# S5 mixer of a two-block transformer: four state units at a time on the TensorE array, and two of VectorE's six modulation operations given to GpSimd

## The chip, the cores and the metric

The kernel runs on one core of one Trainium2 chip. The metric is device time in microseconds (us) of one execution, the median of several runs. The change is judged against the kernel before.

## The reference

The program is two transformer blocks over 512 tokens of width 1024 in float32. The second block has three mixers side by side (RWKV-7, S5, gated linear attention), then cross attention and a convolutional feed-forward. The change touches only S5, a complex diagonal state space model with 32 groups of 16 channels and 64 states each:

```
bu_re = einsum('blgc,gnc->blgn', uf, bbar_re)
bu_im = einsum('blgc,gnc->blgn', uf, bbar_im)
_, _, s_re, s_im = lax.associative_scan(_complex_affine_combine,
                       (abar_re, abar_im, bu_re, bu_im), axis=1)
y = (einsum('blgn,gcn->blgc', s_re, c_re) - einsum('blgn,gcn->blgc', s_im, c_im) + d * uf)
y = gelu(y)
y = y * sigmoid(y @ w_glu + b_glu)
```

## The kernel before

The weights of both blocks stream from memory as 512 KB units through a ring of five buffers in SBUF. SyncE issues these loads as the ring comes free. TensorE works almost without a break; the other engines prepare what it reads and take away what it wrote. One stage of the program, `s5_inputs`, holds the S5 recurrence together with the projections of the second block.

The S5 states are worked as units of 128 partitions (two channel groups, 64 states each). There are 16 of them for each half of the sequence (256 tokens). VectorE takes them two at a time: one q is two units (index e) over one half a, so q runs from 0 to 15. In the rest of this text such a q is called a pair.

For a pair, the steps are:

- `inputs(q)` on TensorE, L2772 to L2784: bu for both units, real and imaginary part. That is 4 matmuls with a contraction of 32 rows. The two units sit in two different 32-row groups of the array. Each matmul writes 256 columns of a PSUM bank. The pair takes banks 0 and 1 or banks 2 and 3, in turn.
- The modulation on VectorE, L2888 to L2895: four products of bu with cosine and sine tables (`er`, `ei`), and then a sum and a difference of these products. Each is 128 partitions by 512 elements. The factors come from PSUM and SBUF; the sum and difference read only SBUF.
- Four `tensor_tensor_scan` of 256 elements (L2903), real and imaginary part of two units.
- Four products that turn the scanned states back (L2908 to L2911), into the buffer `o[:, q % 2]`.
- `outputs(q)` on TensorE, L2786 to L2798: 8 matmuls with 32 output columns each, accumulated four deep. The two units write two different 32-partition strips of one bank.
- After every second pair `s5_skip` (L2929) adds d * u and takes the bank's result.

Each float32 matmul shows as two MATMUL and two LDWEIGHTS records in the trace, so 8 matmuls are 16 records.

Between these TensorE issues steps of the projections, from the generator `side`: one step is one 128x512 matmul. There are 120 steps: 88 from `contract_steps` (L1059) and 32 from `token_steps` (L2966). The order is written out by hand:

```
inputs(0)
inputs(1)
for q in range(16):
    for _ in range(8):
        next(side, None)
    outputs(q)
    if q + 2 < 16:
        inputs(q + 2)
```

ScalarE copies the projections out of banks 6 and 7 and applies the gelu at the end. GpSimd has nothing in this stage; its next work is two memsets of the following stage (L3152, L3153), after the last `outputs`. Stages follow each other without a barrier; only semaphores order them.

Of the kernel before, what the change touches and what calls it, by code (L numbers as in the profile page):

```python
# [17 lines left out]
ALU = mybir.AluOpType  # L18
# [309 lines left out]
class Signal:  # L328
# [13 lines left out]
    def now(self):  # L342
# [12 lines left out]
           'r_t', 'r_tok', 'r_tt', 'r_turned', 'r_u', 'r_u0', 'r_u0p', 'r_vb', 'r_w',  # L355
           'r_wp',
           'w_sum', 'w_p', 'w_p1', 'w_u', 'w_c', 'w_c11', 't_sum', 'd_x', 'd_freed', 's5_bt', 'conv_gate', 'conv_up',
           's5_loaded', 's5_in', 's5_mod', 's5_dem', 's5_out', 's5_y', 's5_glu',
           'g_in', 'g_neg', 'g_soft', 'g_cum', 'g_exp', 'g_dec', 'g_turned', 'g_kt', 'g_scored', 'g_att', 'g_intra', 'g_inter',
           'x_p', 'x_add', 'x_g', 'm_in', 'm_sq', 'm_sum', 'm_ln', 'm_root', 'm_ready', 'k_p', 'k_out', 'q_p', 'q_out', 'v_p',  # L360
           'x_sum', 'x_ln', 'x_root', 'prescaled', 'g_upd', 'g_st', 'g_y', 'g_add', 'g_sq', 'g_sum', 'g_ms', 'g_ln', 'g_root', 'g_gate']
# [596 lines left out]
class Net:  # L958
# [1788 lines left out]
    def s5_inputs(self, down, both, square, t, u, y, qk, go, gd, v, m, z, o, cneg):  # L2747
# [12 lines left out]
        with self.phase() as block:  # L2760
            @block.tensor
            def _(pe):
                def columns():
                    for i in range(2, len(dense)):
                        if i == 3:
                            pe.wait_ge(*s['s5_u'].at(2))
                        elif i >= 4:
                            pe.wait_ge(*s['freed'].at(i - 3))
                        yield from self.contract_steps(pe, ps[:, 6 + i % 2, :], h, s['projected'], i == 2)
                    yield from self.token_steps(pe, [6, 7], h, s['projected'], s['freed'], len(dense) - 2)  # L2770

                def inputs(q):  # L2772
                    a, p = pairs[q]
                    if q >= 2:
                        pe.wait_ge(*s['s5_mod'].at(q - 1))
                    if a == 0 and p % 2 == 0:
                        i = p // 2
                        pe.wait_ge(*(s['s5_u'].at(i + 1) if i < 2 else s['freed'].at(i - 1)))
                    for j in range(2):
                        for e in range(2):  # L2780
                            r, i = rows(2 * p + e), p // 2
                            mm = pe.matmul(ps[:, 2 * (q % 2) + e, half * j:half * (j + 1)], t.bt[r, j, i * P:(i + 1) * P],
                                           u[r, i, half * a:half * (a + 1)], start=True, stop=True)
                    mm.then_inc(*s['s5_in'].up())  # L2784

                def outputs(q):  # L2786
                    a, p = pairs[q]
                    i = p // 2
                    pe.wait_ge(*s['s5_dem'].at(q + 1))
                    if p % 2 == 0 and 4 * a + i >= 2:  # L2790
                        pe.wait_ge(*s['s5_y'].at(4 * a + i - 1))
                    c = lambda e: slice(32 * (2 * p + e), 32 * (2 * p + e) + 32)
                    for j in range(4):
                        for e in range(2):
                            w = (t.big[:, 2, c(e)], cneg[:, c(e)], t.big[:, 3, c(e)], t.big[:, 3, c(e)])[j]
                            mm = pe.matmul(ps[rows(2 * p + e), 4 + i % 2, 0:half], w, o[:, q % 2, j, e, :],  # L2796
                                           start=(j == 0), stop=(j == 3))
                    mm.then_inc(*s['s5_out'].up())  # L2798

                down.pe(pe)  # L2800
                self.contract(pe, ps[:, 2, :], h, s['projected'], deferred=True, ready='x_g')
                pe.wait_ge(*s['accumulated'].at(DT - 1))
                self.root_pe(pe, 0)
                pe.matmul(ps[:, 1, :], self.c('ones'), self.root[:, :], start=True, stop=True).then_inc(*s['y_sum'].up())
                pe.wait_ge(*s['d_freed'].at(4))
                self.contract(pe, ps[:, 7, :], h, s['projected'])
                side = columns()
                inputs(0)
                inputs(1)
                for q in range(16):  # L2810
                    for _ in range(8):
                        next(side, None)
                    outputs(q)
                    if q + 2 < 16:
                        inputs(q + 2)
                for _ in side:
                    pass

            self.s5_end, self.y_read = s['s5_out'].at(16), [s['s5_y'].at(7), s['s5_y'].at(8)]
            self.v_read = [s['freed'].at(len(dense) + k) for k in (1, 2)]  # L2820

            @block.scalar
# [25 lines left out]
            def _(dve):  # L2848
# [30 lines left out]
                for k in range(DT):  # L2879
                    dve.tensor_tensor(h[k], h[k], self.root[:, :], ALU.mult).then_inc(*s['prepared'].up())  # L2880
                dve.tensor_scalar(cneg[:, :], t.big[:, 2, :], -1.0, None, ALU.mult).then_inc(*s['vec'].up())
                for q, (a, p) in enumerate(pairs):
                    g = 2 * p
                    er, ei = t.er[:, g:g + 2, :], t.ei[:, g:g + 2, :]
                    dve.wait_ge(*s['s5_in'].at(q + 1))
                    b = 2 * (q % 2)
                    re, im = ps[:, b:b + 2, 0:half], ps[:, b:b + 2, half:2 * half]
                    dve.tensor_tensor(m[:, 0, :, :], re, er, ALU.mult).then_inc(*s['vec'].up())  # L2888
                    dve.tensor_tensor(m[:, 1, :, :], im, ei, ALU.mult).then_inc(*s['vec'].up())
                    dve.tensor_tensor(m[:, 2, :, :], im, er, ALU.mult).then_inc(*s['vec'].up())  # L2890
                    dve.wait_ge(*s['vec'].now())
                    dve.tensor_tensor(m[:, 3, :, :], re, ei, ALU.mult).then_inc(*s['s5_mod'].up())
                    dve.tensor_tensor(m[:, 0, :, :], m[:, 0, :, :], m[:, 1, :, :], ALU.add).then_inc(*s['vec'].up())
                    dve.wait_ge(*s['s5_mod'].at(q + 1))
                    dve.tensor_tensor(m[:, 2, :, :], m[:, 2, :, :], m[:, 3, :, :], ALU.subtract).then_inc(*s['vec'].up())  # L2895
                    dve.wait_ge(*s['vec'].now())
                    if q:
                        dve.wait_ge(*s['s5_dem'].at(q))
                    for j in range(2):
                        for e in range(2):  # L2900
                            mag = t.fac[:, 0, g + e:g + e + 1].to_broadcast([P, half])
                            first = t.init[:, j, g + e:g + e + 1] if a else 0.0
                            dve.tensor_tensor_scan(z[:, j, e, :], mag, m[:, 2 * j, e, :], first, ALU.mult,  # L2903
                                                   ALU.add).then_inc(*s['vec'].up())
                    if q >= 2:
                        dve.wait_ge(*s['s5_out'].at(q - 1))
                    dve.wait_ge(*s['vec'].now())
                    dve.tensor_tensor(o[:, q % 2, 0, :, :], z[:, 0, :, :], er, ALU.mult).then_inc(*s['vec'].up())  # L2908
                    dve.tensor_tensor(o[:, q % 2, 1, :, :], z[:, 1, :, :], ei, ALU.mult).then_inc(*s['vec'].up())
                    dve.tensor_tensor(o[:, q % 2, 2, :, :], z[:, 0, :, :], ei, ALU.mult).then_inc(*s['vec'].up())  # L2910
                    dve.tensor_tensor(o[:, q % 2, 3, :, :], z[:, 1, :, :], er, ALU.mult).then_inc(*s['s5_dem'].up())  # L2911
                    if a == 0:
                        dve.tensor_copy(t.end[:, :, g:g + 2], z[:, :, :, half - 1]).then_inc(*s['vec'].up())
                    if q == 7:
                        self.s5_turn_state(dve, t)
                    if q >= 2 and p % 2 == 0:
                        self.s5_skip(dve, q // 2 - 1, u, y)
                self.s5_skip(dve, 7, u, y)

            @block.sync  # L2920
            def _(sync):
                self.prefetch(sync)

    def s5_skip(self, dve, k, u, y):

        a, i = divmod(k, 4)
        t = slice(256 * a, 256 * (a + 1))
        dve.wait_ge(*self.s['s5_out'].at(2 * k + 2))
        dve.scalar_tensor_tensor(out=y[:, i, t], in0=u[:, i, t], scalar=self.v('s5_d', i), in1=self.ps[:, 4 + i % 2, 0:256],  # L2929
                                 op0=ALU.mult, op1=ALU.add).then_inc(*self.s['s5_y'].up())  # L2930

# [403 lines left out]
    def second_block(self, down, both, square):  # L3335
        p = self.place
        y_s5, y_gla, qk, go = (p(n, [P, 4, S], 8 * i) for i, n in enumerate(('y_s5', 'y_gla', 'gla_qk', 'gla_go')))
        gd, v, u = p('gla_gd', [P, S], 32), p('gla_v', [P, 4, S], 34), p('u_s5', [P, 4, S], 42)
        self.s5_inputs(down, both, square, self.s5_tables, u, y_s5, qk, go, gd, v, p('s5_m', [P, 4, 2, 256], 50), p('s5_z', [P, 2, 2, 256], 58),
                       p('s5_o', [P, 2, 4, 2, 256], 62), p('s5_cneg', [P, S], 78))  # L3340
        rkv, low = p('rkv', [P, 12, S], 50), p('low_rw', [P, 2, S], 74)
        self.gla_beside_rwkv(u, y_s5, y_gla, qk, go, gd, v, rkv, low)
# [73 lines left out]
```

## Time and profile before

| | us |
|---|---|
| median of 3 runs | 2916.47 (2916.03 to 2916.61) |
| profiled execution, its own time | 2917.33 |
| span of its trace | 2916.0 |
| TensorE matmul busy | 2858.7 (98%) |
| TensorE weight load busy | 1961.6 (67%) |
| VectorE busy | 1619.2 (56%) |
| ScalarE busy | 652.4 (22%) |
| GpSimd busy | 5.0 (0%) |

The spans of the engines overlap. PE is the matmul part of TensorE, PEld its weight load, DVE is VectorE, ACT is ScalarE, POOL is GpSimd and SP is SyncE. A share of 98% holds for the whole span; the stage of the change lies between 1574.9 and 1737.6 us.

### The profile page before, as it was taken

What the parts mean: (1) busy time and instruction counts of PE and PEld (TensorE: products, weight loads), DVE (VectorE), ACT (ScalarE), POOL (GpSimd) and SP (SyncE); (2) the same over time, 40 slices, a digit from 0 to 9 for tenths busy, and PEclk for the clock granted to TensorE, in tenths of its full rate; (3) what the DMA queues carried; (4) which work ended last, traced back from release to release, by engine and by line L of the source; (5) the groups of instructions that cost most, each with busy time, mean ns of one, the idle gap of its engine ahead of it and who ended that gap; (6) DMA issues with size and microseconds to landing.
All of it is one profiled execution on the core that took longest, in us unless ns stands there. A gap on an engine that the chain in (4) does not pass through costs nothing.

```text
span 2916.0 us, 36187 instructions
## 1 busy us (share of the span) xinstructions
PE 2858.7 (98%) x14760; PEld 1961.6 (67%) x14760; DVE 1619.2 (56%) x3196; ACT 652.4 (22%) x1347; POOL 5.0 (0%) x22
## 2 busy tenths in 40 slices
PE   8999999999999999999998999999999999999998
PEld 3567588888544575888885445455554875688886
DVE  5675544453336855466746984455452633666654
ACT  5651300000136513100000021422220102222200
POOL 0000000000000000000000000000000000000000
PEclk9999999999999999999999999999999999999999
DMA  4013122222211231222221111211112331222222
GB/s 146 29 51 101 51 94 87 87 99 97 80 60 49 73 109 66 94 73 87 88 100 65 51 58 58 72 45 45 45 45 93 110 108 46 78 90 89 88 87 80
DMA packets 61941, 224.25 MB, mean 77 GB/s; under 512 B 6992, under 2 KB 7248, under 8 KB 61264
## 3 DMA queue, kind: packets, MB, share of 16 engines
q1 hardware_dynamic: 61776, 221.94, 22.7%
q8 instruction: 117, 1.92, 0.3%
q14 instruction: 48, 0.39, 0.0%
HBM read 219.82 MB, written 2.10 MB: 76 GB/s over the span
## 4 chain that ended last, share of the span: by engine, by line
PE 93%; DVE 6%; issue 1%; ACT 0%; DMA 0%; SPq 0%; DVEq 0%; ACTq 0%
PE ps L1636 29%; PE ps L647 18%; PE ps L1059 15%; PE ps L1047 8%; PE ps L1112 4%; PE ps L1418 3%; PE ps L1391 2%; PE ps L1074 2%; PE ps L1403 2%; PE ps L2796 1%; PE ps L2102 1%; PE ps L2123 1%; PE ps L2319 1%; PE ps L2966 1%; PE ps L1717 1%
## 5 line engine op out<-in xcount | busy, mean ns | idle before, releaser
L1059 PE MATMUL ps<-h,ring 128*128 128x512 f32 x784 | 362.5, 606 | 0.0
L1636 PE MATMUL ps<-h,ring 128*128 128x256 f32 x1136 | 270.7, 381 | 8.5 <-DVE u L1658 4.6
L1059 PEld LDWEIGHTS ps<-h,ring 128*128 128x128 f32 x784 | 143.1, 191 | 159.5 <-issue 153.5
L1636 PEld LDWEIGHTS ps<-h,ring 128*128 128x128 f32 x1136 | 215.9, 191 | 44.0 <-issue 8.7
L1636 PE MATMUL ps<-h_sums,w_sums 128*128 128x256 f32 x1008 | 224.4, 379 | 0.0
L1636 PEld LDWEIGHTS ps<-h_sums,w_sums 128*128 128x128 f32 x1008 | 191.5, 190 | 26.0
L647 PE MATMUL ps<-hid_sums,d_sums 128*128 128x256 f32 x720 | 171.2, 379 | 1.0 <-DVE hid_sums L1595 1.0
L647 PEld LDWEIGHTS ps<-hid_sums,d_sums 128*128 128x128 f32 x720 | 136.6, 190 | 20.3 <-issue 1.8
L1577 DVE TENSOR_TENSOR d_sums<-ring 128x512 f32<-128x512 f32 (+1 forms) x48 | 31.5, 656 | 172.0 <-DMA ring<-stream_dram 172.0
L1112 PE MATMUL ps<-o_x,ring 128*128 128x512 f32 x256 | 112.2, 593 | 0.0
L1636 PE MATMUL ps<-c_h_sums,c_sums 128*128 128x256 f32 x504 | 112.2, 379 | 0.0
L757 ACT ACTIVATE d_xsq<-x 128x512 f32<-128x512 f32 x42 | 24.9, 620 | 368.2 <-DVE x L723 368.2
L1403 PEld LDWEIGHTS ps<-constants,probs 128*128 128x128 f32 x560 | 62.4, 140 | 63.1 <-DVE probs L1525 47.5
L1636 PEld LDWEIGHTS ps<-c_h_sums,c_sums 128*128 128x128 f32 x504 | 95.8, 190 | 13.0
L1457 ACT ACTIVATE probsT<-ps 128x512 f32<-128x512 f32 (+2 forms) x176 | 82.8, 508 | 96.3 <-PE ps L1403 95.8
L1047 PE MATMUL ps<-h,ring 128*128 128x512 f32 x224 | 97.6, 592 | 0.0
L1403 PE MATMUL ps<-constants,probs 128*128 128x128 f32 x560 | 82.7, 279 | 10.4 <-DVE probs L1525 9.6
L1112 PEld LDWEIGHTS ps<-o_x,ring 128*128 128x128 f32 x256 | 48.3, 190 | 60.8 <-issue 58.8
L647 PE MATMUL ps<-hid_sums,ring 128*128 128x256 f32 x360 | 85.5, 379 | 0.0
L647 PE MATMUL ps<-hid,ring 128*128 128x256 f32 x352 | 82.5, 379 | 0.0
L647 PE MATMUL ps<-hid,d_sums 128*128 128x256 f32 x352 | 82.5, 379 | 0.0
L3302 DVE SCALAR_TENSOR_TENSOR c_conv<-c_x,vectors,c_conv 128x511 f32<-128x511 f32 (+1 forms) x88 | 62.1, 747 | 34.1 <-ACT c_conv L3254 33.3
(613 smaller groups left out, 4739.3 us busy)
## 6 DMA issues: line engine op xcount, KB each, us to landing
ring<-stream_dram SPq DMA_DIRECT2D x395, 512.0 KB, 3.7
bias<-bias_dram SPq DMA_DIRECT2D x8, 448.0 KB, 4.3
mem<-mem_dram SPq DMA_DIRECT2D x3, 1024.0 KB, 5.0
x<-x_dram SPq DMA_DIRECT2D x4, 512.0 KB, 7.5
out_dram<-x SPq DMA_DIRECT2D x8, 256.0 KB, 2.2
rope_ab<-ropes_dram SPq DMA_DIRECT2D x4, 256.0 KB, 8.6
s_big<-s_big_dram SPq DMA_DIRECT2D x1, 1024.0 KB, 6.9
constants<-constants_dram SPq DMA_DIRECT2D x1, 768.0 KB, 11.5
```

Of the source, the lines that this page charges most:

```text
L647: mm = pe.matmul(self.region(q, at), w(j), x(k), start=opens, stop=last and j == len(ks) - 1, skip_group_check=True)
L1047: mm = pe.matmul(out, w, r, start=(k == 0), stop=(k == len(rhs) - 1))
L1059: mm = pe.matmul(out, w, r, start=(k == 0), stop=(k == len(rhs) - 1))
L1074: mm = pe.matmul(out, l, w, start=(k == 0), stop=(k == len(lhs) - 1))
L1112: mm = pe.matmul(self.ps[:, m % 4, :], self.next_block(pe), src[k], start=(k == 0), stop=(k == len(src) - 1))
L1391: mm = pe.matmul(ps[:, bank(u, j), 0:(k1 - k0) * P], gr.q[j][i][:, qt * P:(qt + 1) * P], gr.k[j][i][:, k0 * P:k1 * P], start=(i == 0), sto ...
L1403: mm = pe.transpose(ps[:, turn_bank(u, j), b * P:(b + 1) * P], pr[:, u % 3, j, b * P:(b + 1) * P], self.c('ident'))
L1418: mm = pe.matmul(ps[at:at + rows, to, c], gr.v(b, j)[i], pt[:, p % 2, j, b, c], start=(b == 0), stop=(b == nk - 1), skip_group_check=True)
L1457: ins = act.activation(pt[:, p % 2, j, k0:k1, qt * P:(qt + 1) * P], ps[:, turn_bank(u, j), 0:(k1 - k0) * P].rearrange("p (b q) -> p b q", ...
L1577: dve.tensor_tensor(s1, a21, a22, ALU.add).then_inc(*s['vec'].up())
L1636: mm = pe.matmul(ps[:, bank + at, 0:256], w(k), x(k), start=start and k == 0, stop=k == 3, skip_group_check=not start)
L3302: ins = dve.scalar_tensor_tensor(out=out, in0=xs[:, f % 2, j, 0:S - lag], scalar=self.v('conv', (2 - lag) * 2 * FT + FT * j + f), in1=out, ...
```

## The change

TensorE's S5 work is grouped by four units (n from 0 to 7) in place of two. `inputs(n)` issues 8 matmuls over four row groups and fills banks 0 to 3; `outputs(n)` issues 16 matmuls over four column groups. The number of matmuls is the same, and so is the work of VectorE's pairs apart from the following. Its four products are issued one pair ahead of the scans (`turned_inputs(q + 1)` before the scans of q), into a second buffer `m[1]` of 8 KB per partition. The sum and the difference are issued by GpSimd, which signals `s5_add`. The waits change accordingly: `inputs(n)` waits for all products of the four units before, `outputs(n)` for both pairs of its group, the turning-back products of a pair for the `outputs` that read the whole of `o` before, and `s5_skip` for `outputs` of its group.

```diff
-                def inputs(q):
-                    a, p = pairs[q]
-                    if q >= 2:
-                        pe.wait_ge(*s['s5_mod'].at(q - 1))
-                    if a == 0 and p % 2 == 0:
-                        i = p // 2
+                def inputs(n):
+                    a, i = divmod(n, 4)
+                    if n:
+                        pe.wait_ge(*s['s5_mod'].at(8 * n))
+                    if a == 0:
                         pe.wait_ge(*(s['s5_u'].at(i + 1) if i < 2 else s['freed'].at(i - 1)))
                     for j in range(2):
-                        for e in range(2):
-                            r, i = rows(2 * p + e), p // 2
-                            mm = pe.matmul(ps[:, 2 * (q % 2) + e, half * j:half * (j + 1)], t.bt[r, j, i * P:(i + 1) * P],
-                                           u[r, i, half * a:half * (a + 1)], start=True, stop=True)
+                        for e in range(4):
+                            mm = pe.matmul(ps[:, e, half * j:half * (j + 1)], t.bt[rows(e), j, i * P:(i + 1) * P],
+                                           u[rows(e), i, half * a:half * (a + 1)], start=True, stop=True)
                     mm.then_inc(*s['s5_in'].up())
-                def outputs(q):
...
-                    pe.wait_ge(*s['s5_dem'].at(q + 1))
-                    if p % 2 == 0 and 4 * a + i >= 2:
-                        pe.wait_ge(*s['s5_y'].at(4 * a + i - 1))
+                def outputs(n):
+                    i = n % 4
+                    pe.wait_ge(*s['s5_dem'].at(2 * n + 2))
+                    if n >= 2:
+                        pe.wait_ge(*s['s5_y'].at(n - 1))
+                    c = lambda e: slice(32 * (4 * i + e), 32 * (4 * i + e) + 32)
                     for j in range(4):
-                        for e in range(2):
+                        for e in range(4):
                             w = (t.big[:, 2, c(e)], cneg[:, c(e)], t.big[:, 3, c(e)], t.big[:, 3, c(e)])[j]
-                            mm = pe.matmul(ps[rows(2 * p + e), 4 + i % 2, 0:half], w, o[:, q % 2, j, e, :],
+                            mm = pe.matmul(ps[rows(e), 4 + i % 2, 0:half], w, o[:, e // 2, j, e % 2, :],
                                            start=(j == 0), stop=(j == 3))
                     mm.then_inc(*s['s5_out'].up())
...
                 inputs(0)
-                inputs(1)
-                for q in range(16):
-                    for _ in range(8):
+                for n in range(8):
+                    for _ in range(6 if n == 0 else 2):
                         next(side, None)
-                    outputs(q)
-                    if q + 2 < 16:
-                        inputs(q + 2)
+                    if n < 7:
+                        inputs(n + 1)
+                    for _ in range(10 if n == 0 else 14):
+                        next(side, None)
+                    outputs(n)
...
+                def turned_inputs(q):
+                    mq, g, b = m[q % 2], 2 * pairs[q][1], 2 * (q % 2)
+                    er, ei = t.er[:, g:g + 2, :], t.ei[:, g:g + 2, :]
+                    dve.wait_ge(*s['s5_in'].at(q // 2 + 1))
+                    re, im = ps[:, b:b + 2, 0:half], ps[:, b:b + 2, half:2 * half]
+                    for j, (x, y) in enumerate(((re, er), (im, ei), (im, er), (re, ei))):
+                        dve.tensor_tensor(mq[:, j, :, :], x, y, ALU.mult).then_inc(*s['s5_mod'].up())
+
+                dve.wait_ge(*s['vec'].now())
+                turned_inputs(0)
                 for q, (a, p) in enumerate(pairs):
...
-                    dve.tensor_tensor(m[:, 3, :, :], re, ei, ALU.mult).then_inc(*s['s5_mod'].up())
-                    dve.tensor_tensor(m[:, 0, :, :], m[:, 0, :, :], m[:, 1, :, :], ALU.add).then_inc(*s['vec'].up())
-                    dve.wait_ge(*s['s5_mod'].at(q + 1))
-                    dve.tensor_tensor(m[:, 2, :, :], m[:, 2, :, :], m[:, 3, :, :], ALU.subtract).then_inc(*s['vec'].up())
                     dve.wait_ge(*s['vec'].now())
+                    if q < 15:
+                        turned_inputs(q + 1)
+                    dve.wait_ge(*s['s5_add'].at(2 * q + 2))
...
                     if q >= 2:
-                        dve.wait_ge(*s['s5_out'].at(q - 1))
+                        dve.wait_ge(*s['s5_out'].at(q // 2))
...
+            @block.gpsimd
+            def _(pool):
+                for q in range(16):
+                    mq = m[q % 2]
+                    pool.wait_ge(*s['s5_mod'].at(4 * q + 4))
+                    pool.tensor_tensor(mq[:, 0, :, :], mq[:, 0, :, :], mq[:, 1, :, :], ALU.add).then_inc(*s['s5_add'].up())
+                    pool.tensor_tensor(mq[:, 2, :, :], mq[:, 2, :, :], mq[:, 3, :, :], ALU.subtract).then_inc(*s['s5_add'].up())
...
-        dve.wait_ge(*self.s['s5_out'].at(2 * k + 2))
+        dve.wait_ge(*self.s['s5_out'].at(k + 1))
```

## Rows read from the trace of the kernel before

**Rows 1.** The page: busy time, and the chain that ended last by engine.

```profile
PE 2858.7 (98%) x14760; PEld 1961.6 (67%) x14760; DVE 1619.2 (56%) x3196; ACT 652.4 (22%) x1347; POOL 5.0 (0%) x22
...
PE 93%; DVE 6%; issue 1%; ACT 0%; DMA 0%; SPq 0%; DVEq 0%; ACTq 0%
```

**Rows 2.** Stretches: length, busy us of each engine (records), granted clock, DMA share, GB/s.

```profile
1600.00:1620.00 20.00, 20.00 (x81) 8.99 (x81) 19.16 (x34) 1.19 (x2) 0.00 (x0) 1.00 0.13 42
...
1700.00:1720.00 20.00, 20.00 (x82) 8.98 (x81) 18.35 (x30) 1.19 (x2) 0.00 (x0) 1.00 0.03 10
```

**Rows 3.** The chain that ended last, 1600 to 1720: start us, us, what.

```profile
1603.86 1.85 PE ps L2796 x16
1605.71 1.06 PE ps L2782 x8
1606.77 7.06 PE ps L1059 x16
```

**Rows 4.** Waits, 1560 to 1745: us in total, times, longest.

```profile
DVE s_m L2888 <- PE ps L2782: 7.3, 12, 1.0
...
PE ps L2796 <- DVE s_o L2911: 5.1, 2, 4.8
```

**Rows 5.** The same columns as rows 2, after TensorE's first long wait.

```profile
1584.70:1589.40 4.70, 0.02 (x2) 0.02 (x2) 4.67 (x10) 0.55 (x1) 0.00 (x0) 0.88 0.00 0
1589.40:1598.50 9.10, 9.10 (x28) 3.96 (x29) 9.00 (x17) 0.00 (x0) 0.00 (x0) 0.50 0.07 8
1598.50:1603.79 5.29, 5.29 (x14) 2.12 (x12) 5.22 (x10) 0.00 (x0) 0.00 (x0) 1.00 0.22 86
```

**Rows 6.** Timeline, VectorE and TensorE at the start: start us, us, instruction, idle before it.

```profile
1574.91 2.11 PE L2782 MATMUL ps<-u_s,s_bt 32*128 32x256 f32 x16 [2.79 <-DVE u_s L2876]
1575.37 4.90 DVE L2880 TENSOR_TENSOR h<-h,root 128x512 f32<-128x512 f32 x8
...
1580.52 0.68 DVE L2888 TENSOR_TENSOR s_m<-ps,s_er 128x512 f32<-128x512 f32 x1
```

**Rows 7.** Timeline, one pair of VectorE with a skip.

```profile
1598.11 0.69 DVE L2888 TENSOR_TENSOR s_m<-ps,s_er 128x512 f32<-128x512 f32 x1
...
1600.64 0.68 DVE L2893 TENSOR_TENSOR s_m<-s_m 128x512 f32<-128x512 f32 x1
...
1601.95 2.44 DVE L2903 TENSOR_TENSOR_SCAN s_z<-s_fac,s_m 128x256 f32<-128x256 f32 x4
...
1604.49 0.69 DVE L2908 TENSOR_TENSOR s_o<-s_z,s_er 128x512 f32<-128x512 f32 x1
...
1606.98 0.47 DVE L2929 SCALAR_TENSOR_TENSOR y_s<-u_s,vectors,ps 128x256 f32<-128x256 f32 x1
...
1607.37 0.68 DVE L2888 TENSOR_TENSOR s_m<-ps,s_er 128x512 f32<-128x512 f32 x1
```

**Rows 8.** Timeline of matmuls, another stage: four 64 by 64 tiles of the array.

```profile
1912.16 0.22 PE L2364 MATMUL ps<-constants,pair 64*64 64x64 f32 x1
1912.17 0.22 PE L2365 MATMUL ps<-pair,constants 64*64 64x64 f32 x1
1912.17 0.22 PE L2364 MATMUL ps<-constants,pair 64*64 64x64 f32 x1
1912.18 0.22 PE L2365 MATMUL ps<-pair,constants 64*64 64x64 f32 x1
1912.22 0.22 PE L2364 MATMUL ps<-constants,pair 64*64 64x64 f32 x1
```

**Rows 9.** Groups of GpSimd over the whole span: busy us, mean ns.

```profile
L1375 POOL COPY shaped<-sinks 128x2 f32<-128x2 f32 x16 | 2.9, 186 | 175.0 <-DVE sinks L1481 93.5 <-ACT probs L1472 81.5
L3153 POOL MEMSET gla_att<- 128x2048 f32 x1 | 1.8, 1805 | 0.0
```

**Rows 10.** The end of the stage: timeline of matmuls.

```profile
1735.73 0.63 PE L2796 MATMUL ps<-s_o,s_big 128*32 128x256 f32 x4 [0.32 <-DVE s_o L2911]
...
1737.58 0.70 PE L1047 MATMUL ps<-gla_gd,ring 128*128 128x512 f32 x1
```

More of the change, by code:

```diff
@@ L357 @@
            'w_sum', 'w_p', 'w_p1', 'w_u', 'w_c', 'w_c11', 't_sum', 'd_x', 'd_freed', 's5_bt', 'conv_gate', 'conv_up',
-           's5_loaded', 's5_in', 's5_mod', 's5_dem', 's5_out', 's5_y', 's5_glu',
+           's5_loaded', 's5_in', 's5_mod', 's5_add', 's5_dem', 's5_out', 's5_y', 's5_glu',
            'g_in', 'g_neg', 'g_soft', 'g_cum', 'g_exp', 'g_dec', 'g_turned', 'g_kt', 'g_scored', 'g_att', 'g_intra', 'g_inter',
@@ L2784, in inputs @@
                     mm.then_inc(*s['s5_in'].up())
-                def outputs(q):
-                    a, p = pairs[q]
-                    i = p // 2
-                    pe.wait_ge(*s['s5_dem'].at(q + 1))
-                    if p % 2 == 0 and 4 * a + i >= 2:
-                        pe.wait_ge(*s['s5_y'].at(4 * a + i - 1))
-                    c = lambda e: slice(32 * (2 * p + e), 32 * (2 * p + e) + 32)
+                def outputs(n):
[4 more added lines that the diff above has]
+                    c = lambda e: slice(32 * (4 * i + e), 32 * (4 * i + e) + 32)
@@ L2808, in _ @@
                 inputs(0)
-                inputs(1)
-                for q in range(16):
-                    for _ in range(8):
+                for n in range(8):
+                    for _ in range(6 if n == 0 else 2):
                         next(side, None)
-                    outputs(q)
-                    if q + 2 < 16:
-                        inputs(q + 2)
+                    if n < 7:
[3 more added lines that the diff above has]
+                    outputs(n)
                 for _ in side:
                     pass
-            self.s5_end, self.y_read = s['s5_out'].at(16), [s['s5_y'].at(7), s['s5_y'].at(8)]
+            self.s5_end, self.y_read = s['s5_out'].at(8), [s['s5_y'].at(7), s['s5_y'].at(8)]
             self.v_read = [s['freed'].at(len(dense) + k) for k in (1, 2)]
@@ L2884, in _ @@
                     er, ei = t.er[:, g:g + 2, :], t.ei[:, g:g + 2, :]
[L2885 to L2890, printed above, removed]
-                    dve.wait_ge(*s['vec'].now())
-                    dve.tensor_tensor(m[:, 3, :, :], re, ei, ALU.mult).then_inc(*s['s5_mod'].up())
-                    dve.tensor_tensor(m[:, 0, :, :], m[:, 0, :, :], m[:, 1, :, :], ALU.add).then_inc(*s['vec'].up())
-                    dve.wait_ge(*s['s5_mod'].at(q + 1))
-                    dve.tensor_tensor(m[:, 2, :, :], m[:, 2, :, :], m[:, 3, :, :], ALU.subtract).then_inc(*s['vec'].up())
-                    dve.wait_ge(*s['vec'].now())
+                    dve.wait_ge(*s['vec'].now())
+                    if q < 15:
+                        turned_inputs(q + 1)
+                    dve.wait_ge(*s['s5_add'].at(2 * q + 2))
                     if q:
@@ L2902, in _ @@
                             first = t.init[:, j, g + e:g + e + 1] if a else 0.0
-                            dve.tensor_tensor_scan(z[:, j, e, :], mag, m[:, 2 * j, e, :], first, ALU.mult,
+                            dve.tensor_tensor_scan(z[:, j, e, :], mag, m[q % 2][:, 2 * j, e, :], first, ALU.mult,
                                                    ALU.add).then_inc(*s['vec'].up())
                     if q >= 2:
-                        dve.wait_ge(*s['s5_out'].at(q - 1))
+                        dve.wait_ge(*s['s5_out'].at(q // 2))
                     dve.wait_ge(*s['vec'].now())
@@ L3338, in second_block @@
         gd, v, u = p('gla_gd', [P, S], 32), p('gla_v', [P, 4, S], 34), p('u_s5', [P, 4, S], 42)
-        self.s5_inputs(down, both, square, self.s5_tables, u, y_s5, qk, go, gd, v, p('s5_m', [P, 4, 2, 256], 50), p('s5_z', [P, 2, 2, 256], 58),
+        self.s5_inputs(down, both, square, self.s5_tables, u, y_s5, qk, go, gd, v, [p(f's5_m{j}', [P, 4, 2, 256], (50, 88)[j]) for j in range(2)], p('s5_z', [P, 2, 2, 256], 58),
                        p('s5_o', [P, 2, 4, 2, 256], 62), p('s5_cneg', [P, S], 78))
```

## The prediction

> **What bounds the kernel now.** I read the page's busy shares and its chain first: TensorE is busy for 98% of the span and makes up 93% of the chain that ended last [rows 1]. Time is saved only where TensorE gets less to do or waits less. Next come the stretches of the stage: from 1600 on TensorE is busy for 20.00 of every 20 us, at full clock, while VectorE has 18.4 to 19.2 [rows 2]. So TensorE sets the pace and VectorE follows close behind. The list of waits agrees: 12 times VectorE waited for `inputs` (7.3 us), and TensorE waited for VectorE's states for 5.1 us, 4.8 of them once, at the start [rows 4]. The chain then gives the pace of one pair: `outputs` 1.85 us, `inputs` 1.06 us, eight projection steps 7.06 us, together 9.97 us [rows 3], or 19.94 us for four units. The steps alone are 8 x 0.854 = 6.83 us (two records each, 0.427 us apart), so 0.23 us goes into changing over. After the first wait the granted clock was 0.50 for the 9.1 us from 1589.4 [rows 5], that is 1.2 of 2.4 GHz; about half of it, 4.6 us, is lost.
>
> **What four groups are worth.** The 16 records of an `outputs` start within 1.85 us. A 128x256 float32 record that had the array alone would take half of the 0.427 us of a 512 column one, 0.213 us, and 16 of them 3.4 us. So today two run side by side. With four column groups the 32 records of four units are again 8 waves of 0.216 us: 1.85 us for four units in place of 3.70. In the same way `inputs` is 1.06 in place of 2.12 us. No row of this kernel has four 32-wide groups at once. The nearest are the 64x64 tiles of another stage: four matmuls start within 0.02 us and the next four 0.06 us later [rows 8]. Four tiles with their weight loads do run together, and the array takes the instructions faster (eight records in 0.06 us) than is wanted here (eight in 0.216). I take the full overlap. The bounds are none, 3.7 and 1.06 + 0.87 = 1.93 us, and full, 1.85 and 1.06 us. The number of steps stays at 120, and so does the number of stretches of steps (15). Removed from TensorE's work: 8 x 1.85 + 8 x 1.06 = 23.3 us.
>
> The Trainium skill ("TensorE: Matmul & The Clock Gate", Part 3) gives 3.07 times for four row groups, not 4. By that rule, as an estimate, a wave would last 0.28 in place of 0.216 us, and 96 waves would give back 6 us; the pairs here reach a full 2 times, and no row shows four.
>
> **The start.** VectorE's first product begins at 1580.52, behind the eight products for h [rows 6]. Now `inputs(1)` needs the products of two pairs, since banks 0 to 3 are all in use: 2 x 2.45 us (2.53 today [rows 7], less a wait that goes), to 1585.5. TensorE has only `inputs(0)` and six steps before it, which end at about 1579.8, so it waits 5.7 us. At the second place, `outputs(0)` needs two whole pairs. In VectorE's order these are the products of three pairs, the scans of two (2.54 us each) and two turnings back (2.45 each) [rows 7]: 1580.52 + 3 x 2.45 + 5.1 + 4.9 = about 1598. By then TensorE, at half clock for some 9 us as in [rows 5], is with its ten steps until 1599.7, so this wait is covered. Loss at the start: 0.4 + 5.7 + 4.7 = 10.8 us. Today the stage has 162.7 us from 1574.91 to 1737.58 [rows 6, 10], of which 102.5 are steps, 29.6 `outputs`, 17.0 `inputs`, 3.4 change-overs; 10.2 are lost. So the start costs 0.6 us more than now. It also ends with eight steps ahead of `outputs(7)`, which remove today's last wait of 0.3 us [rows 10]. With TensorE as the bound the stage gains 23.3 - 0.6 + 0.3 = 23.0 us.
>
> **The new waits in the steady part.** Four units now take 16 x 0.854 + 0.46 + 1.85 + 1.06 = 17.03 us of TensorE. Let `inputs(n)` end at T. VectorE does products, scans and turning back of a pair by T + 7.5, the next products by T + 9.9, the next scans by T + 12.5. TensorE does 14 steps to T + 12.2, and `outputs(n-1)`, whose states came 4.7 us before, to T + 14.1. VectorE's turning back has to wait for this end, since it overwrites `o`: 1.6 us of idle time, with its scans' successors queued behind it. It then has 2.45 + 0.39 (skip) left and is at T + 17.0 where `inputs(n+1)` ends (T + 17.03). That loop closes without a wait of TensorE as long as VectorE's slack of 1.6 us in four units holds. The products for `inputs(n+1)` are read 6 us before. The stage's own transfers (0.03 to 0.13 DMA share [rows 2]) are far from binding. What waits behind the stage (ScalarE's gelu, then GpSimd's memsets) moves with it, and TensorE has filler work there, so the gain is passed on.
>
> **What GpSimd costs.** VectorE loses the sum and the difference: 1600.64 to 1601.95, 1.31 us a pair, and 0.12 us of wait in the products [rows 7]: 8.87 becomes about 7.5 us. GpSimd has no two-input operation in the trace. Its memset of 2048 elements took 1.805 us, so 512 elements are 0.45 us; that is the lower bound of an addition. Two reads and a write each at that pace are 1.35 us, the upper one [rows 9]. A pair has two: 0.9 to 2.7 us. They begin as VectorE begins the scans of the pair before, and are wanted only 7.4 us later, so their own length is hidden (for the first pair there are 2.4 us, so at most 0.3 us are seen). What is not hidden is what they may take from VectorE, as both read SBUF; call it c, us per pair. Bounds: 0, and the whole of GpSimd's time, 2.7. VectorE's total from 1580.52: 16 x 7.5 + 7 x 0.39 + 0.8 (turning the state between the halves) + 0.8 (slower scans there) = 124.3, and `outputs(7)` after it: the stage would end at 1707 + 16c if VectorE bounds it. TensorE's bound is 1714.6. So c below 0.5 costs nothing, at 1.2 the gain is 11 us, and at 1.9 it is gone. I take c = 0.6: the scans need 0.61 us for 256 elements where a product takes as much for 512 [rows 7], so they fetch half as densely as a product, and I charge a quarter of the worst. That gives 1716.6 and a gain of 21.0 us.
>
> The Trainium skill speaks against this step ("SBUF — State Buffer", Who interferes with whom): VectorE with two inputs in SBUF contends with a GpSimd instruction that reads SBUF, and the pair of ports that they share is described as an exclusive lock. "GPSIMD Engine Reference" (Elementwise) has 4497 ns for an addition of 2048 elements, which as an estimate is 1.12 us for 512 and 2.25 for the two. A lock of that length would end the stage at 1743, 5.4 us later than now, against 21 us earlier by my charge. No row shows the two engines together.
>
> **Sum.** 2917.33 (the profiled execution's own time, 1.3 over its span, 0.9 over the median) - 21.0 = 2896.3, and 0.9 lower as a median: 2895.5 us. Faster or slower by 0.2% is 5.8 us, about what can be told from no change here.
>
> **The rivals.**
> - *TensorE or a small c bounds the stage* (forecast), chance 0.58: c up to 1, end at 1714.6 to 1723, time 2893.5 to 2902. For it: rows 8, and the scans' sparse fetching. Own range 2891 to 2902.
> - *VectorE becomes the bound by contention*, c from 1 to 1.9: gain 14 to 0, time 2902 to 2916. Chance 0.17. For it: VectorE's slack is only 1.6 us in four units, and the additions lie exactly beside scans that read two SBUF operands.
> - *The additions cost VectorE their full length*: c over 1.9, from which point the kernel is slower; at 2.25 it is 2922, at the bound of 2.7 1750 or 12.6 us later, 2929. Then moving them off VectorE (-1.4 us a pair) is undone and more. Chance 0.13.
> - *Four groups don't run side by side*: without overlap in `outputs` and `inputs` four units take 13.66 + 0.46 + 3.7 + 1.93 = 19.75 us against 19.94, gain about 3 us, time 2913; with one of the two, 2900.5 (only `inputs` without it: 7 us lost) or 2908 (only `outputs`: 14.8 lost). Against it: rows 8. Chance 0.12.
>
> The chance of slower by over 0.2% is the upper part of the third case (c above 2.27) with a little for mishaps: 0.12. Within 0.2% are the ends of the second, the start of the third and part of the fourth: 0.11. Faster 0.77. The range for 8 in 10 runs from 2891 (c of 0 and no loss at the start beyond the 0.6 us) to 2917, which leaves out the slower case.
>
> **What would show it.** `outputs` as 32 records in about 1.85 us, in starts of four; `inputs` as 16 in 1.06. TensorE's chain with 17.0 us for four units, `outputs(7)` ending near 1716. One wait of 5 to 6 us before `inputs(1)`, and half clock for some 9 us behind it. The scans at 0.61 us apart (c = 0) or longer, the turning-back products at 0.605 or longer, and GpSimd's additions at 0.5 to 1.4 us. I would be wrong if the scans were stretched by over 0.15 us each (4 scans, c = 0.6), if starts of four came 0.4 us apart, or if TensorE waited for `s_o` in every group.

## The result and the profile after

The changed kernel took 2919.12 us (median of 20 runs, 2917.73 to 2920.74) against 2916.05 us for the kernel before (20 runs); the ratio is 1.0012, 95% interval 1.0006 to 1.0017. It is slower by about 3 us where 21 us of gain were forecast.

The changed trace, timeline of TensorE, VectorE and GpSimd in two pairs of the steady part (weight loads and projection steps left out):

```profile
1622.77 0.64 PE L2793 MATMUL ps<-s_o,s_big 128*32 128x256 f32 x8
...
1623.22 0.61 PE L2793 MATMUL ps<-s_o,s_cneg 128*32 128x256 f32 x8
...
1623.65 1.05 PE L2793 MATMUL ps<-s_o,s_big 128*32 128x256 f32 x16
...
1625.23 4.48 DVE L2903 TENSOR_TENSOR_SCAN s_z<-s_fac,s_m 128x256 f32<-128x256 f32 x4
1625.39 1.58 POOL L2925 TENSOR_TENSOR s_m<-s_m 128x512 f32<-128x512 f32 x1 [6.41 <-DVE s_m L2886]
...
1626.55 1.15 PE L2780 MATMUL ps<-u_s,s_bt 32*128 32x256 f32 x16
1626.92 1.65 POOL L2926 TENSOR_TENSOR s_m<-s_m 128x512 f32<-128x512 f32 x1
...
1629.81 0.69 DVE L2908 TENSOR_TENSOR s_o<-s_z,s_er 128x512 f32<-128x512 f32 x1
```

TensorE's groups of four came as forecast. `outputs` now has 32 records, which begin at 1622.77 and end at 1624.70, about as long as 16 took [rows 3]; `inputs` has 16 in 1.15 us. VectorE's part did not come as forecast: the four scans take 4.48 us where they took 2.44 [rows 7]. The same four, asked one by one:

```profile
1625.23 0.68 DVE L2903 TENSOR_TENSOR_SCAN s_z<-s_fac,s_m 128x256 f32<-128x256 f32 x1
...
1625.82 1.69 DVE L2903 TENSOR_TENSOR_SCAN s_z<-s_fac,s_m 128x256 f32<-128x256 f32 x1
...
1627.43 1.69 DVE L2903 TENSOR_TENSOR_SCAN s_z<-s_fac,s_m 128x256 f32<-128x256 f32 x1
...
1629.04 0.66 DVE L2903 TENSOR_TENSOR_SCAN s_z<-s_fac,s_m 128x256 f32<-128x256 f32 x1
```

Two scans are as they were and two take 1.69 us. Read beside GpSimd's rows, they take turns: the first addition begins under the first scan and ends at 1626.97, the second scan is issued at 1625.82 and ends 0.54 us after that; the second addition then outlasts this scan and ends at 1628.57, and the third scan ends 0.55 us later. So c, the time that the additions take from VectorE, is 4.48 - 2.44 = 2.0 us a pair. Fifteen of the 16 pairs pay it; the last pair's scans have no additions beside them and take 2.67 us.

The change makes VectorE the bound. The stretch from 1600 to 1734 (columns as in [rows 2]) and the chain that ended last show it. The chain's rows for the scans have all four in one:

```profile
1600.00:1734.00 134.00, 117.75 (x528) 50.86 (x528) 132.25 (x187) 10.71 (x17) 41.84 (x26) 0.95 0.17 52
```
```profile
1663.16 1.88 DVE s_m L2886 x3
1665.03 4.53 DVE s_z L2903 x4
...
1670.26 0.69 DVE s_o L2909
...
1672.46 2.48 DVE s_m L2886 x4
1674.94 4.53 DVE s_z L2903 x4
```

TensorE, which had no free time in the stretches of [rows 2], is now busy for 117.75 of 134 us, and VectorE for 132.25. The waits of TensorE after the change (us in total, times, longest):

```profile
PE ps L2793 <- DVE s_o L2911: 18.7, 6, 6.1
...
PE ps L2780 <- DVE s_m L2886: 2.3, 1, 2.3
```

The longest of them also costs clock. Before `outputs(7)` TensorE sat idle for 6.1 us. Its 32 records then took 3.64 us on the chain, not 1.86, at a granted clock of 0.50, that is 1.2 of 2.4 GHz:

```profile
1736.03:1739.61 3.58, 3.58 (x33) 1.39 (x33) 0.00 (x0) 0.00 (x0) 0.00 (x0) 0.50 0.02 5
```

`outputs(0)` ran at 0.50 too, after 5.2 us of idle time, but VectorE's pace hides that one.

I measure the stage from the first `inputs` to the first matmul of the next stage (L1047 on gla_gd): 1574.9 to 1737.6 before [rows 6, 10], 162.7 us; 1575.9 to 1739.6 after, 163.7 us. So the stage is 1.0 us longer. Another 0.7 us is lost in the four records behind it, which took 2.62 us on the chain where they took 1.91, the first of them still at 0.50. The stage also starts 1.0 us later, though nothing ahead of it was changed. That is scatter between executions: in the traces of this document it starts between 1574.1 and 1576.4, and twice the same kernel gave 1574.13 and 1575.18.

### The profile page after: what moved, and what is told of

The parts are those of the page before. It is cut to its first block and busy times, and to the rows that moved or that the text cites. A ratio compares the mean times of both kernels' runs of the same rounds, so it can differ in the third digit from the quotient of the medians.

```text
span 2918.3 us, 36204 instructions
## 1 busy us (share of the span) xinstructions
PE 2844.2 (97%) x14760; PEld 1953.3 (67%) x14760; DVE 1626.4 (56%) x3164; ACT 652.8 (22%) x1347; POOL 55.3 (2%) x54
## 5 line engine op out<-in xcount | busy, mean ns | idle before, releaser
L1047 PE MATMUL ps<-h,ring 128*128 128x512 f32 x224 | 97.6, 592 | 0.0
```

What stands on the lines that cost most here:

```text
L1047: mm = pe.matmul(out, w, r, start=(k == 0), stop=(k == len(rhs) - 1))
```

## The experiments

All times are medians of 4 to 10 runs, beside 13 runs of the kernel before on the same chip (medians 2915.4 to 2916.1 us). Line numbers differ by a few between kernels.

### The sums back on VectorE

```diff
-            @block.gpsimd   (the whole block)
+                    dve.tensor_tensor(mq[:, 0, :, :], mq[:, 0, :, :], mq[:, 1, :, :], ALU.add)...
+                    dve.tensor_tensor(mq[:, 2, :, :], mq[:, 2, :, :], mq[:, 3, :, :], ALU.subtract)...
                     dve.wait_ge(*s['s5_add'].at(2 * q + 2))
```

> The changed kernel with the sum and the difference back on VectorE, right before the scans; groups of four units, two product buffers and all orders stay. Theory A (GpSimd's additions stretch VectorE's scans, which fetch two operands from SBUF; nothing else is lost): the four scans of a pair fall from 4.5 to 2.5 us and 1.3 us of sums come in, so a pair of VectorE takes about 9.1 in place of 9.7 us, VectorE still sets the pace, and the time is about 2909 us (10 us under the changed kernel, 7 under the one before). Theory B (the loss is in the new waits of groups of four: fewer PSUM buffers, outputs only after two pairs): VectorE's work per pair is then what it was before and the waits come on top, so 2916 us or more.

Measured: 2909.32 us, ratio 0.9978 (0.9969 to 0.9988). The scans are back, and VectorE still sets the pace:

```profile
L2907 DVE TENSOR_TENSOR_SCAN s_z<-s_fac,s_m 128x256 f32<-128x256 f32 x32 | 19.5, 673 | 0.3
```
```profile
PE ps L2793 <- DVE s_o L2915: 12.5, 5, 5.6
```

So undoing only the move to GpSimd is 10 us faster than the whole change, as the first theory said. The loss is not in the waits of the groups of four. These groups, with the products one pair ahead, are worth 6.5 us by themselves. They would be worth more if VectorE kept up.

### No sums at all

```diff
-            @block.gpsimd   (the whole block)
-                    dve.wait_ge(*s['s5_add'].at(2 * q + 2))
+                    dve.wait_ge(*s['s5_mod'].at(4 * q + 4))
```

> The changed kernel without the sum and the difference on any engine: the scans read the first and third product directly (this part of the computation is left out). It measures the limit with no load on GpSimd at all. Theory A: scans at 0.61 us each, TensorE sets the pace with 17.0 us for four units, TensorE's only long wait is the one before the second inputs; the stage ends 24 us earlier than in the changed kernel, 2895 us. Theory B: TensorE goes on waiting in every group, 2910 us or more.

Measured: 2895.23 us, ratio 0.9929 (0.9915 to 0.9944). This kernel leaves the sum and the difference out of the computation, so it shows the limit of the design and not a gain to be had. The steady part is TensorE's, with 17.07 us from one group's steps to the next:

```profile
1603.23 12.21 PE ps L1059 x28
...
1620.30 12.21 PE ps L1059 x28
...
1637.37 12.21 PE ps L1059 x28
```

Two later groups took 18.02 us. In each of them TensorE waited 0.7 us for ScalarE, which had yet to copy a projection out of PSUM; the kernel before had no such wait:

```profile
1677.54 2.84 PE L2966 MATMUL ps<-ring,h 128*128 128x512 f32 x6 [0.69 <-ACT gla_gd L2837]
```

### The sums beside the products

```diff
                     pool.wait_ge(*s['s5_mod'].at(4 * q + 4))
+                    if q:
+                        pool.wait_ge(*s['s5_dem'].at(q))
```

> The changed kernel with one wait more on GpSimd: the additions of a pair start only when the turning back of the pair before is done, so they run beside the next pair's four products (one operand from PSUM, one from SBUF) in place of the scans (two from SBUF). Theory A (contention only where VectorE reads two SBUF operands): scans back at 0.61 us, products at 0.60, additions 1.23 us apart as in the first pair, so the scans wait for the second addition by about 0.2 us a pair; VectorE's pair is 7.8 us and TensorE sets the pace: 2896 to 2899 us. Theory C (any work of GpSimd beside any work of VectorE costs it): the products stretch in place of the scans, and with 2.5 us of additions beside 2.4 us of products the pair takes 9.3 us or more: 2913 us or more.

Measured: 2899.41 us, ratio 0.9944 (0.9929 to 0.9959), at the upper end of what the first theory expected. One wait more on GpSimd takes 20 us off the changed kernel. The same two additions per pair, the same operands, now beside products that read one operand from PSUM:

```profile
L2886 DVE TENSOR_TENSOR s_m<-ps,s_er 128x512 f32<-128x512 f32 x32 | 21.9, 685 | 0.4 <-PE ps L2780 0.2
...
L2903 DVE TENSOR_TENSOR_SCAN s_z<-s_fac,s_m 128x256 f32<-128x256 f32 x32 | 19.5, 673 | 0.6 <-POOL s_m L2928 0.2
```
```profile
L2928 POOL TENSOR_TENSOR s_m<-s_m 128x512 f32<-128x512 f32 x16 | 20.4, 1274 | 0.0
L2927 POOL TENSOR_TENSOR s_m<-s_m 128x512 f32<-128x512 f32 x16 | 20.3, 1272 | 1492.7 <-DVE s_m L2886 1406.0 <-DVE s_o L2911 86.6
```

Neither side is stretched: the products keep their 0.685 us, and the additions fall from 1.57 and 1.62 us to 1.27. One of each, side by side:

```profile
1639.95 1.28 POOL L2928 TENSOR_TENSOR s_m<-s_m 128x512 f32<-128x512 f32 x1
1640.24 0.68 DVE L2886 TENSOR_TENSOR s_m<-ps,s_er 128x512 f32<-128x512 f32 x1
```

This trace also has the clearest single row. Between the halves VectorE turns the state with products of 128x16 that read two SBUF tensors; here they met the additions:

```profile
1646.58 0.17 DVE L2948 TENSOR_TENSOR s_init<-s_end,s_fac 128x16 f32<-128x16 f32 x1
1646.61 1.28 POOL L2927 TENSOR_TENSOR s_m<-s_m 128x512 f32<-128x512 f32 x1 [5.38 <-DVE s_o L2911]
...
1646.67 1.24 DVE L2949 TENSOR_TENSOR s_turn<-s_end,s_fac 128x16 f32<-128x16 f32 x1
...
1647.84 0.16 DVE L2950 TENSOR_TENSOR s_init<-s_end,s_fac 128x16 f32<-128x16 f32 x1
```

The second is as small as the first, and takes 1.24 us in place of 0.17: it ends within 0.02 us of the addition. Sixteen elements are a 32nd of the addition's 512, so a shared bandwidth would not hold them up for that long; what they wait for is the whole instruction.

### Memsets in place of the sums

```diff
-                    pool.tensor_tensor(...)  (both)
+                    for k in range(3):
+                        if k:
+                            pool.wait_ge(*s['s5_add'].at(3 * q + k))
+                        pool.memset(mq[:, 1::2, :, :], 0.0).then_inc(*s['s5_add'].up())
```

> The additions are replaced by three memsets of 1024 elements per pair at the same place, beside the scans; they only write, into the second and fourth product's space, and the sum and the difference are left out of the computation. Theory A (it is GpSimd's reading that contends with VectorE's second operand): scans stay at 0.61 us although GpSimd is busy for about 2.9 us beside them, and the time is that of the kernel without sums, 2895 us. Theory C (any GpSimd access): scans at 1.2 to 1.7 us as in the changed kernel, 2915 to 2920 us.

Measured: 2894.23 us, ratio 0.9928 (0.9913 to 0.9943), within 1 us of the kernel without sums. The sum and the difference are left out here too. GpSimd is busy beside the scans for about as long as with the additions, and the scans keep their time:

```profile
1623.83 2.43 DVE L2903 TENSOR_TENSOR_SCAN s_z<-s_fac,s_m 128x256 f32<-128x256 f32 x4
1623.97 2.97 POOL L2928 MEMSET s_m<- 128x1024 f32 x3 [4.83 <-DVE s_m L2886]
```

Over the whole stage:

```profile
L2928 POOL MEMSET s_m<- 128x1024 f32 x48 | 45.6, 951 | 1479.3 <-DVE s_m L2886 1477.5
```
```profile
L2903 DVE TENSOR_TENSOR_SCAN s_z<-s_fac,s_m 128x256 f32<-128x256 f32 x32 | 19.4, 672 | 0.7 <-POOL s_m L2928 0.7
```

So GpSimd's activity as such costs nothing, nor do its writes. What the additions have and the memsets lack is their reads, and their arithmetic; no run here parts these two.

### The sums beside the turning back

The last scan of a pair signals `s5_scan`, and GpSimd's additions wait for it.

```diff
                     pool.wait_ge(*s['s5_mod'].at(4 * q + 4))
+                    if q:
+                        pool.wait_ge(*s['s5_scan'].at(q))
```

> The changed kernel with the additions released when the scans of the pair before are done, so they run beside the four turning-back products, which also read two operands from SBUF. Theory L (a lock: an instruction of VectorE with two SBUF operands waits until GpSimd's running addition has ended, and the other way round): the scans are back at 0.61 us apart, two of the four products take about 1.7 us instead of 0.69 and the other two are as before, the additions take about 1.6 us, and the time is again 2917 to 2921 us. Rival S (the port's bandwidth is shared): all products that overlap are stretched by about the same factor, the additions too. Rival (only scans suffer, by their slow recurrence): products as before and 2897 us or so.

Measured: 2921.47 us, ratio 1.0021 (1.0012 to 1.0031), close to what the lock expected. The scans are at 0.67 us again, and now two of the four products pay. The rows of VectorE and GpSimd in one pair:

```profile
1618.27 1.77 POOL L2928 TENSOR_TENSOR s_m<-s_m 128x512 f32<-128x512 f32 x1 [6.50 <-DVE s_z L2903]
...
1618.82 1.76 DVE L2910 TENSOR_TENSOR s_o<-s_z,s_ei 128x512 f32<-128x512 f32 x1
...
1619.99 1.71 POOL L2929 TENSOR_TENSOR s_m<-s_m 128x512 f32<-128x512 f32 x1
...
1620.50 1.75 DVE L2911 TENSOR_TENSOR s_o<-s_z,s_ei 128x512 f32<-128x512 f32 x1
```

So it is not the slow recurrence of a scan that suffers. The instruction with two SBUF operands that comes next waits for the addition under way, and the next addition waits for it. The two products end 0.54 and 0.55 us after an addition ends, as the two slow scans of the changed kernel did. The bandwidth rival would have stretched all that overlap by one factor.

### The moved sums without the groups of four

The kernel before, with the products one pair ahead and the additions beside the products, as above; TensorE's groups and order as before.

> The kernel before with one part of the change alone, in the good place: products one pair ahead, second product buffer, sum and difference on GpSimd beside the products; TensorE keeps its groups of two units and its order. Theory A (TensorE bounded the kernel before, so a faster VectorE is worth nothing by itself): four units still take 19.9 us of TensorE, VectorE's idle time grows, the first outputs come about 0.7 us later because two pairs' products go ahead of the first scans; 2916 to 2918 us. Rival (VectorE's 1.4 us a pair was what the kernel waited for): up to 20 us less.

Measured: 2936.63 us, ratio 1.0072 (1.0055 to 1.0088). It is 21 us slower than the kernel before, and both theories missed. VectorE waited for TensorE 14 times:

```profile
DVE s_m L2888 <- PE ps L2782: 42.2, 14, 5.7
```

I had not followed the order. The products of q+2 stand on VectorE before the scans of q+1, and need `inputs(q+2)`, which stands on TensorE behind `outputs(q)`. Its chain goes round in 10.6 us a pair (1627.86 to 1638.45) in place of 9.97: `outputs`, `inputs`, products, scans, turning back, one after another. The exchange of two lines tests this:

```diff
-                    outputs(q)
                     if q + 2 < 16:
                         inputs(q + 2)
+                    outputs(q)
```

> The kernel of the moved sums alone, groups of two units, with one exchange in TensorE's order: inputs of the pair after next come before the outputs, not behind them. Theory D (that kernel lost 21 us because two engines stepped in turn: the products run one pair ahead, so they wait for inputs that stand behind outputs, which wait for VectorE's last product): now the inputs need only products that are long done, VectorE no longer waits for TensorE's outputs, four units take TensorE's 19.9 us again and the time is that of the kernel before, 2914 to 2918 us. This is then also the fair test of the moved sums alone: no gain by themselves. Rival (the loss came from GpSimd or from the later first scans): it stays at 2930 us or more. Rival (a faster VectorE alone is a gain): under 2910 us.

Measured: 2923.51 us, ratio 1.0025 (1.0015 to 1.0036). The exchange takes back 14 of the 21 us. The explanation holds for the middle, the expected time does not. From 1603 to 1724 the chain is TensorE's alone with 9.97 us a pair, so moving the sums gives nothing there, but the end is later and the kernel remains 7 us slower than the one before:

```profile
1604.42 1.85 PE ps L2796 x16
1606.27 7.06 PE ps L1059 x16
1613.34 1.06 PE ps L2782 x8
1614.40 1.85 PE ps L2796 x16
```
```profile
1740.00 1.07 PE L2796 MATMUL ps<-s_o,s_big 128*32 128x256 f32 x4 [5.09 <-DVE s_o L2913]
```

For the last pair there are no products to hide the additions behind, the scans wait 2.3 us for them, TensorE 5.1 us, and it then runs `outputs` in 3.63 us on the chain, at a granted clock of 0.50.

### The tail mended

The kernel of "The sums beside the products", with the scans of each part waiting for their own addition, the last pair's sums on VectorE one pair early, and the ninth pair's additions behind the turned state.

```diff
+                    if q == 14:
+                        mq = m[1]
+                        dve.wait_ge(*s['s5_mod'].at(64))
+                        (the sum and the difference of pair 15, on VectorE)
                     for j in range(2):
+                        if q < 15:
+                            dve.wait_ge(*s['s5_add'].at(2 * q + 1 + j))
...
+                    if q == 8:
+                        pool.wait_ge(*s['s5_mod'].at(37))
```

> The kernel with the additions beside the products, mended at three places seen in its trace: the scans of the real part wait for their own addition only; the last pair, which has no products to run beside, gets its sum and difference from VectorE while it waits for outputs anyway; and the ninth pair's additions start behind the small operations that turn the state. Theory A (the 4 us between it and the kernel without sums are TensorE's 3.6 us wait before the last outputs, and the half clock behind it): that wait falls under 1.5 us and the time is 2895 to 2897 us. Rival (the 4 us come from GpSimd's work in every pair): 2898 us or more.

Measured: 2895.98 us, ratio 0.9935 (0.9920 to 0.9949). TensorE's waits for the states, which had a longest of 3.6 us in the kernel it mends:

```profile
PE ps L2793 <- DVE s_o L2917: 2.0, 2, 1.1
```

This gives back 3.4 of the 4.2 us that lay between it and the kernel without sums, as expected. The turns show once more: VectorE's own sum for the last pair, issued at 1699.85 while an addition ran to 1700.31, took 1.01 us in place of 0.68 and ended 0.55 us after it.

> The mended kernel once more beside it, for a narrower interval: 2895 to 2897 us, a ratio of 0.993 to the kernel before.

Measured: 2896.27 us, ratio 0.9932 (0.9920 to 0.9944). It does the whole computation and is 20 us faster than the kernel before and 23 us faster than the changed one.

## Why the prediction was wrong

The step that failed is the size of c in "What GpSimd costs": "I take c = 0.6 ... I charge a quarter of the worst". It measured 2.0 us. The reason that I gave for it, that the scans fetch half as densely, assumes that the two engines share bandwidth. The turns of the scans, the 128x16 product of 1.24 us and the turning-back products of 1.75 us show turns of whole instructions, for which density doesn't matter. The signs that the prediction named for this came: the scans were stretched by 0.5 us each in the mean, not by 0.15, and TensorE waited for `s_o` in six of eight groups.

The sum around c held. VectorE's work from its first product to its last was put at 124.3 us without c. With 15 x 2.0 us that is 154.3, and 154.4 were measured (1581.59 to 1735.98). The sum's end of 1707 + 16c gives 1739 for c = 2.0, a stage of 164.1 us from 1574.9, against 163.7 measured. That this is so close is in part luck: only 15 pairs paid, 2.0 us less, and `outputs(7)` at half clock took 1.8 us more, which the sum did not have. The stage is 22.0 us longer than the forecast's 141.7. The larger c (15 x 2.0 in place of 16 x 0.6) makes 20.4 of them, and the half clock 1.8. The time missed by 23.6 us; what remains lies outside the stage, 0.7 us of it right behind.

**The third rival** was the right one ("the additions cost VectorE their full length", chance 0.13), with its break-even point. It is not quite the full length: an addition alone took 1.23 us from start to start, and a scan caught by one lost 1.03 us. From the end of one slow scan (1627.51) to the end of the addition behind it (1628.57) are 1.06 us. Spans on GpSimd are rough, but VectorE's instruction ended 0.54 or 0.55 us behind the addition each time that is quoted here for instructions of 256 or more elements. The range ended at 2917, where c is 1.9, and the result lies 2 us beyond it.

The Trainium skill's rule that I set beside the sum ("SBUF — State Buffer", Who interferes with whom) was weighed too low. By it VectorE's instructions with two SBUF inputs contend with a GpSimd instruction that reads SBUF, and not with one that only writes it. The runs agree: scans of 0.66 us took 1.69 beside additions and 0.67 beside memsets. The estimate from the Trainium skill ("GPSIMD Engine Reference", Elementwise), 1.12 us for an addition of 512 elements, is a little below the 1.23 us measured.

**Four groups side by side**: right. `outputs` took 1.86 and `inputs` 1.08 us on the chain for twice the units. A group of four came every 17.07 us where 17.03 was forecast, in every kernel in which VectorE keeps up, but for the two groups that waited for ScalarE. By the 3.07 times that the Trainium skill ("TensorE: Matmul & The Clock Gate", Part 3) gives for four row groups, `inputs` would, as an estimate, have taken 1.06 x 4 / 3.07 = 1.38 us; the 1.08 measured are close to the full 4 times. The price of the rival that lost was wrong: without any overlap the prediction's own losses of 7 and 14.8 us leave 1.2 us of its 23.0, so about 2915 us and not 2913.

**The bound of TensorE**: right in size. Forecast for c near 0 was 2893.5 us, the kernel without sums took 2895.2. Its stage has 139.4 us where 139.7 was forecast, but some parts of it offset each other, as follows.

**The start**: wrong in its parts, and charged too high. I had six steps end at about 1579.8 and a wait of 5.7 us before `inputs(1)`, with 9 us of half clock behind it. In the changed kernel the 12 records of six steps ran from 1577.06 to 1584.17, the first 3.6 us of them at a granted clock of 0.53, and the wait was 2.3 us. Six steps are 5.1 us by the prediction's own price of a step, so they could not have ended at 1579.8; it shows no working for that time. In the kernel without sums the two stretches of half clock at the start are about 3.4 us each. There `outputs(0)` begins 23.0 us after the first `inputs`, where the prediction has 24.8.

**The steady waits**: right. In the kernel without sums VectorE's turning back waited for `outputs` (7.1 us in 5 waits, the longest 2.3), and TensorE in the middle never for VectorE. The two waits for ScalarE, which made two groups 18.02 us long, were not in the prediction and cost 1.9 us.

**The end**: the gain of 0.3 us did not come. TensorE waits before the last `outputs` in every kernel with groups of four, 6.1 us in the changed one and 1.1 in the mended one. In the kernel without sums VectorE has a turning back, a skip, four scans and another turning back to do after `outputs(6)`, about 8 us, and TensorE eight steps of 6.8 in all.

What stays open: why two of four instructions are caught and not three (two additions, two victims, fits the turns, but which side wins a race was not tried), and whether an operation of GpSimd with one SBUF input locks in the same way. That it is the additions' reads that lock, and not something else in which they differ from memsets, is the likely reading, but no run shows it by itself.

## What to carry to other kernels

Before work is moved to GpSimd, list what VectorE does at that moment. Beside operations with a PSUM operand GpSimd's additions were free here, beside operations with two SBUF operands each took about 1 us from VectorE. With groups of four, moving them was worth 10 us in the one place and cost 10 us in the other, against leaving them on VectorE. A second price is the tail: the last unit has nothing to hide behind, so let the fast engine do that one. And when products are put one unit ahead on one engine, write down for the other engine which issue they now wait for; an unchanged order there cost 14 us.

## What the runs showed of the hardware

- A GpSimd addition with two SBUF inputs, 128x512 float32, took 1.27 us (1.23 from start to start), and about 1.6 to 1.7 us when it took turns with VectorE.
- VectorE instructions with two SBUF inputs and such an addition took turns by whole instructions: a scan of 0.66 us took 1.69, a product of 0.69 took 1.75, a 128x16 product of 0.17 took 1.24. A product with one PSUM operand stayed at 0.685, and scans beside GpSimd memsets at 0.67.
- Four 32-column groups with four different 128-row streams run beside each other without loss: 32 records in 1.86 us on the chain where two groups had 16 in 1.85; four 32-row groups: 16 in 1.08 where two had 8 in 1.06.
- After TensorE had been idle for 6.1 us, the 32 records of `outputs(7)` ran at a granted clock of 0.50 (1.2 GHz) and took 3.64 us in place of 1.86.
